# ScalarE takes a unit's root and a gate's copy of the combined projection ahead of the block's copy

## The chip, the cores and the metric

The kernel runs on one core of one Trainium2 chip. The metric is the device time of one launch, in microseconds (us). The engines are named TensorE (PE in the rows), VectorE (DVE), ScalarE (ACT), GpSimd (POOL) and SyncE (SP, which here only issues DMAs). PEld is TensorE's loading of weights.

## What is computed

One step of a trunk of two layers over 512 latent tokens and 128 prompt tokens, all in float32, with a width of 1024. The part that the change touches is the combined projection of a layer and what hangs on it:

```python
h = rms_norm(x, p['norm1_g'][l]) * (1 + scale1) + shift1
proj = h @ p['w_in'][l]
gq, gk, gv, gg, gaf, gab, cval, cgate, aq, ak, av = jnp.split(proj, ...)
la_f = jax.nn.log_sigmoid((gaf @ p['gla_a_w_f'][l] + p['gla_a_b_f'][l])) / GLA_NORMALIZER
la_b = jax.nn.log_sigmoid((gab @ p['gla_a_w_b'][l] + p['gla_a_b_b'][l])) / GLA_NORMALIZER
u = cval * jax.nn.sigmoid(cgate)              # then a depthwise convolution of 31 taps
qa = rms_norm(heads(aq, HEAD_DIM), p['q_norm_g'][l])
ka = rms_norm(heads(ak, HEAD_DIM), p['k_norm_g'][l])
...                                           # rotary on latent tokens, softmax attention
...                                           # gated linear attention by chunks of 64 tokens
```

After attention, the chunked linear attention and the convolution, an output projection and a gated residual follow, and then a mixture of single experts: each token picks 16 of 16384 experts in each of 8 heads, and the rows of these experts are gathered from two tables in memory.

## The kernel before

Each layer goes through four phases: projection with attention, chunked linear attention, output projection, expert stage. All four compute engines meet at the end of a phase (line 257); output projection and experts are one phase for this. Activations are kept transposed: 128 channels on the partitions and 640 tokens along the free dimension.

The projection is cut into 16 blocks of output columns, numbered 0 to 15 and listed in BLOCKS: the convolution's gate and value (blocks 0 to 3), the attention's key (block 4), its queries (5 to 8), the 32 columns of the two decay gates (9), the keys and queries of the linear attention (10 to 13) and its output gate (14, 15). For each block TensorE runs 16 matmuls into one of two pairs of PSUM banks, taken in turn. The trace has 32 records for them. Before block b it waits until ScalarE has evacuated block b-2 (proj_ev). All matmuls go through one helper, line 561, and so have that line in the profile; transposes are on lines 623 to 846.

Keys and queries form five units (UNITS, u = 0 to 4, which are blocks 4 to 8). Each is normalised per head and, for latent tokens, rotated. A unit's way goes through four engines and shares one buffer at each step:

- ScalarE squares it (line 1009, `square`), in round b = u + 4,
- TensorE averages the squares over each head (`variance`), behind the matmuls of block u + 5, into the first pair of banks. It waits for the square and, from unit 1 on, for the root of the unit before, which empties those banks,
- ScalarE takes the root (line 1015, `deviation`), in round b = u + 6. From unit 1 on it waits until VectorE has normalised the unit before (n_ready), because the roots share the tile SD,
- VectorE takes the reciprocal of the root and scales the unit (lines 1316 and 1317), which sets n_ready,
- TensorE multiplies it with the rotation matrix (`rotated`), behind block u + 7, and VectorE combines the two with cosine and sine (lines 1321 to 1323).

The four decay gates are matmuls of block 9 with a small matrix, behind the matmuls of blocks 11 to 14, into the same first pair of banks. Gate i waits, from the second on, until ScalarE has copied gate i - 1 with its bias (line 1029, z_ready), which it does in round 12 + i.

In layer 0 the blocks from 3 on are each followed by a chunk of the modulation, the product of the conditioning with 512 columns of a weight matrix. SyncE loads a slab of 2 MB for each: it waits until the chunk before is done (m_ps), then issues four DMAs (lines 349 and 350), and after ScalarE has copied the chunk's result (line 973) it writes it to memory in four small DMAs (line 361). For 4 of the chunks the result is turned into columns by TensorE instead, at the beginning of the next chunk, and copied by line 968. SyncE also loads the weights of block b + 3 when block b is done (line 367).

Beside this, VectorE and GpSimd run the two halves of the convolution, VectorE 18 of its taps before it turns to the units and the rest after them; GpSimd all of its taps in one go. After block 15 TensorE duplicates the keys into the layout of attention. It waits there for the last rotation, for the fourth gate's copy and, in layer 0, for the last chunk.

ScalarE runs everything in the order in which the code issues it. A round b of its loop in the projection (lines 1017 to 1035) is before the change: wait for the block's matmuls, copy of the block (line 1020), root, square, gate, and in layer 0 the chunk's result. Sigmoid, Sqrt and Silu each need another activation table than the one before; the table's load is an instruction of its own.

Of the kernel before, what the change touches and what calls it, by code (L numbers as in the profile page):

```python
# [9 lines left out]
ACT = mybir.ActivationFunctionType  # L10
# [7 lines left out]
NTOK = N_SAMPLE + N_PROMPT  # L18
# [26 lines left out]
def group_of(t):  # L45

    return 0 if t < NT_S else 1


def build(nc, x_prompt, x_sample, c, cache_k, cache_v, state_gla, c_ctx, ada_w, ada_b, norm1_g, norm2_g,  # L50
# [4 lines left out]
    with ctx:  # L55
# [3 lines left out]
        def sem(name):  # L59
            return ctx.enter_context(nc.semaphore(name))  # L60
# [133 lines left out]
        def pair(i):  # L194

            return PSF[:, 1024 * i:1024 * i + 1024]

        def zp(i):
# [4 lines left out]
        S = {n: sem(n) for n in (  # L203

            "const_in", "cond_in", "x_in", "adab_in", "gain1_in", "gain2_in", "gate_in", "mod2_in", "vec_in",
            "wv_in", "ck_in", "misc_in", "st_in", "keys_in", "wq_in",

            "cond_zero", "cond_ready", "m_ps", "m_row_done", "mod_out", "mc_ps", "mc_done", "mc_ready",

            "ss_done", "ms_done", "sd_done", "h_ready", "ht_ps", "ht_act", "ht_dve", "vec_ps", "vec_ready", "proj_ps",  # L210
            "proj_ev", "vt_ps", "vt_ready", "kc_ps", "kc_ready", "sq_ready", "var_ps", "sd_ready", "n_ready",
# [55 lines left out]
        NB = len(BLOCKS)  # L267
# [12 lines left out]
        def in_project(b):  # L280

            return b - FIRST_MOD if FIRST_MOD <= b < NB else None
# [20 lines left out]
        NU = len(UNITS)  # L303
# [649 lines left out]
        def _(act):  # L953
# [9 lines left out]
            def mod_rows(bank, n):  # L963

                if n - 1 in COLS:
                    c = n - 1 - COLS[0]
                    act.wait_ge(S["mc_ps"], WIDE + c + 1)
                    act.activation(mod_col[:, 1, 4 * c:4 * c + 4, :],
                                   PS[:, bank, 256:264].rearrange("p (j g) -> p j g", j=4), ACT.Copy)\
                        .then_inc(S["mc_done"], 1)  # L970
                act.wait_ge(S["m_ps"], WIDE + n + 1)
                act.wait_ge(S["mod_out"], 64 * stored(n))
                act.activation(m_chunk, PS[:, bank, 0:P], ACT.Copy).then_inc(S["m_row_done"], 1)

            def project(l):
                for t in range(NT):
                    st.link(act.activation(hbuf[:, t % 2, :], X[:, t, :], ACT.Square, accum_out=sumsq[:, 0, t:t + 1]))
                act.sem_inc(S["ss_done"], 1)
                act.wait_ge(S["ms_done"], l + 1)
                act.activation(rms[:, 0:NT], rstd[:, 0:NT], ACT.Sqrt).then_inc(S["sd_done"], 1)  # L980
                def h_out(t):
                    act.wait_ge(S["mc_ready"], l + 1)
                    act.wait_ge(S["ht_ps"], NT * l + t + 1)
                    for k in range(KT // 2):
                        c = mod_col[:, l, :, group_of(t)]
                        m = act.activation(HT[:, k, P * t:P * t + P], pair(t % 2)[:, P * k:P * k + P], ACT.Identity,
                                           bias=c[:, k:k + 1], scale=c[:, KT + k:KT + k + 1])
                    m.then_inc(S["ht_act"], 1)

                def vectors_out():  # L990
                    act.wait_ge(S["vec_ps"], l + 1)
                    act.activation(vec[:, :], PS[:, 4, 0:R_END], ACT.Copy).then_inc(S["vec_ready"], 1)
                    act.wait_ge(S["kc_ps"], l + 1)
                    act.activation(KC, PS[:, 5, 0:P], ACT.Copy).then_inc(S["kc_ready"], 1)

                if l:
                    vectors_out()
                for t in range(2):
                    h_out(t)
                if l == 0:  # L1000
                    vectors_out()
                for t in range(2, NT):
                    h_out(t)

                def square(u):
                    if u:
                        act.wait_ge(S["var_ps"], NU * l + u)
                    act.wait_ge(S["proj_ev"], NB * l + 4 + u + 1)
                    act.activation(SQ, UNITS[u][0], ACT.Square).then_inc(S["sq_ready"], 1)

                def deviation(u):
                    act.wait_ge(S["var_ps"], NU * l + u + 1)
                    if u:
                        act.wait_ge(S["n_ready"], NU * l + u)
                    act.activation(SD, pair(0)[:, 0:NTOK], ACT.Sqrt, bias=eps_c[:, 0:1]).then_inc(S["sd_ready"], 1)  # L1015

                for b, (dst, w, _c) in enumerate(BLOCKS):
                    act.wait_ge(S["proj_ps"], NB * l + b + 1)
                    f = ACT.Sigmoid if b in (0, 2) else ACT.Silu if b >= NB - 2 else ACT.Copy
                    act.activation(dst, pair(2 + b % 2)[0:w, 0:NTOK], f).then_inc(S["proj_ev"], 1)  # L1020
                    if 0 <= b - 6 < NU:
                        deviation(b - 6)
                    if 0 <= b - 4 < NU:
                        square(b - 4)
                    if b >= 12:
                        i = b - 12
                        col = (R_ABF if i < 2 else R_ABB) + i % 2
                        act.wait_ge(S["z_ps"], 4 * l + i + 1)
                        act.activation(LA[:, i, :], pair(0)[:, 0:NTOK], ACT.Identity, bias=vec[:, col:col + 1])\
                            .then_inc(S["z_ready"], 1)  # L1030
                    if b == 14:
                        act.wait_ge(S["kout_ps"], l + 1)
                        act.activation(KOUT, PS[:, 2, 0:P], ACT.Copy).then_inc(S["kout_ready"], 1)
                    if l == 0 and in_project(b) is not None:
                        mod_rows(3, in_project(b))
# [196 lines left out]
            for l in range(DEPTH):  # L1232
                project(l)
                attention(l)
                phase_end(act, PH * l + 1)
                gla(l)
                phase_end(act, PH * l + 2)
                out_project(l)
                peer(l)
                phase_end(act, PH * l + 3)  # L1240
# [390 lines left out]
```

## Time and profile before

| | us |
|---|---|
| median of 3 runs | 4506.6 |
| lowest and highest | 4503.03, 4546.3 |
| the profiled execution, time | 4498.38 |
| its span | 4496.2 |

| engine | busy us | share of the span |
|---|---|---|
| TensorE, matmuls | 2957.0 | 66% |
| TensorE, weight loads | 1278.9 | 28% |
| VectorE | 2770.1 | 62% |
| ScalarE | 966.7 | 21% |
| GpSimd | 2694.6 | 60% |

The chain that ended last is made of TensorE (25%), DMA (22%), issue (18%), VectorE (17%), GpSimd (15%) and ScalarE (2%). The mean granted clock of TensorE is 0.826 of full speed. In time, the start takes 54 us; the projection of layer 0 lasts from there to 260 us, that of layer 1 from 2318 to 2480 us. Attention and linear attention follow, and the expert stages lie from about 640 to 2300 us and from 2820 us to the end.

How to read the rows: a timeline gives start and duration in us, engine, line, operation, the names and shapes of output and inputs, the number of instructions merged into the row, and in brackets how long the engine was idle before it and who released it. Matmul ends are modelled.

### The profile page before, as it was taken

Reading aid. Unit: us, or ns where it says so; the run is one execution under the profiler, and the core shown is the slowest. Engines: PE = TensorE matmul, PEld = TensorE weight load, DVE = VectorE, ACT = ScalarE, POOL = GpSimd, SP = SyncE. Lnnn points to the kernel's source line nnn. Section 1 sums busy time; section 2 is a strip of 40 time slices with the busy share of each in tenths; the row PEclk is TensorE's granted clock in tenths of the full one; section 3 lists DMA queues with packets and bytes.
Section 4 is the critical chain, followed back from the end, with each engine's and each line's share of the span. In section 5 each row is a group of like instructions: output and inputs, shape, how many; then the busy total and the mean of one; then the engine's idle time right before and its main releaser. Section 6 shows DMA issues by size and latency. Waiting matters only on the chain.

```text
span 4496.2 us, 50088 instructions
## 1 busy us (share of the span) xinstructions
PE 2957.0 (66%) x17386; PEld 1278.9 (28%) x17386; DVE 2770.1 (62%) x6333; ACT 966.7 (21%) x2391; POOL 2694.6 (60%) x2762
## 2 busy tenths in 40 slices
PE   7999845556555555666578998455555556556655
PEld 4567521112221221222134674122212112112211
DVE  3516376677677677667536363766766776776673
ACT  2134111221122122222121422111212221222221
POOL 3700047777777777777748000677777777777775
PEclk9999778887887888777799978688878877888777
DMA  6532259999999999999941103999999999999998
GB/s 220 185 118 92 86 219 409 409 409 405 406 406 406 404 406 405 405 397 409 403 137 35 39 3 109 361 409 409 404 409 404 406 407 402 405 406 407 402 407 341
DMA packets 471181, 1450.20 MB, mean 323 GB/s; under 512 B 54165, under 2 KB 131345, under 8 KB 470801
## 3 DMA queue, kind: packets, MB, share of 16 engines
q0 software_dynamic: 368640, 1342.34, 75.4%
q1 hardware_dynamic: 102290, 104.66, 7.2%
q8 instruction: 140, 2.29, 0.2%
q14 instruction: 111, 0.91, 0.1%
HBM read 1443.62 MB, written 3.21 MB: 322 GB/s over the span
## 4 chain that ended last, share of the span: by engine, by line
PE 25%; DMA 22%; issue 18%; DVE 17%; POOL 15%; ACT 2%; DVEq 1%; SPq 1%; POOLq 0%; ACTq 0%
PE ps L561 24%; DMA arena<-in_peer_u,expert_rows 11%; DMA arena<-in_peer_v,expert_rows 10%; DVE arena L1506 8%; POOL arena L536 8%; POOL arena L544 7%; DVE arena L1454 1%; DVE top_indices L1453 1%; DVE arena L1485 1%; DVE arena L1488 1%; DVE chosen_pair L1490 1%; DVE top_values L1456 1%; DVE best_positions L1453 0%; DMA arena<-in_ada_w 0%; DVE top_indices L1458 0%
## 5 line engine op out<-in xcount | busy, mean ns | idle before, releaser
L561 PE MATMUL ps<-arena 64*64 64x512 f32 (+5 forms) x14768 | 2718.6, 674 | 1423.2 <-issue 1183.6
L1506 DVE CUSTOM_DVE_ANT_0 arena<-arena,ps 128x1024 f32<-128x1024 f32 x1280 | 1526.1, 1218 | 891.3 <-DMA arena<-in_peer_u,expert_rows 883.9
L561 PEld LDWEIGHTS ps<-arena 64*64 64x64 f32 (+2 forms) x14768 | 1121.0, 176 | 3006.7 <-issue 2896.0
L536 POOL DMA_INDIRECT arena<-in_peer_u,expert_rows x1280 | 1218.6, 952 | 688.3 <-issue 318.2
L544 POOL DMA_INDIRECT arena<-in_peer_v,expert_rows x1280 | 1205.9, 942 | 416.9 <-issue 357.9
L1219 ACT ACTIVATE arena<-constants,expert_weight 128x64 f32<-128x64 f32 x1280 | 380.3, 339 | 1370.2 <-PE ps L561 1346.4
L522 POOL MEMSET arena<- 128x4224 f32 x2 | 7.2, 3617 | 380.0 <-ACTq L257 380.0
L1334 DVE TENSOR_REDUCE score_max<-ps 128x1 f32<-128x640 f32 (+1 forms) x80 | 57.2, 716 | 224.5 <-PE ps L561 224.2
L515 POOL TENSOR_SCALAR arena<-arena,vec_columns 128x512 f32<-128x512 f32 x120 | 150.3, 1263 | 10.2 <-issue 10.2
L1146 ACT ACTIVATE arena<-ps 128x256 f32<-128x256 f32 x80 | 30.6, 383 | 477.3 <-PE ps L561 463.5
L1159 ACT ACTIVATE expert_gelu<-expert_act 128x16 f32<-128x16 f32 x80 | 17.3, 216 | 456.6 <-DVE expert_act L1506 456.6
L1506 DVE DVE_READ_ACCUMULATOR2_ANT expert_act<- 128x1 f32 x1280 | 104.3, 82 | 0.0
L518 POOL TENSOR_TENSOR arena<-arena 128x640 f32<-128x640 f32 x60 | 97.3, 1621 | 8.8 <-issue 0.2
L1154 ACT ACT_TABLE_LOAD x78 | 100.1, 1283 | 1.4
L561 PE MATMUL ps<-arena,constants 1*2 1x128 f32 (+3 forms) x404 | 79.9, 428 | 29.0 <-ACT arena L1015 15.4
L1159 ACT ACT_TABLE_LOAD x76 | 97.5, 1283 | 1.3
L525 POOL MEMSET arena<- 128x2048 f32 x2 | 3.6, 1805 | 156.2 <-DVEq L257 156.2
L1020 ACT ACTIVATE arena<-ps 128x640 f32<-128x640 f32 (+1 forms) x32 | 22.5, 702 | 273.9 <-PE ps L561 273.9
L1524 DVE TENSOR_TENSOR arena<-ps,arena 128x1024 f32<-128x1024 f32 x10 | 12.2, 1224 | 112.1 <-PE ps L561 112.1
L1046 ACT ACTIVATE arena<-ps,score_neg_max 128x640 f32<-128x640 f32 (+1 forms) x80 | 56.6, 708 | 108.1 <-DVE score_neg_max L1335 105.1
L1306 DVE SCALAR_TENSOR_TENSOR arena<-arena,vec_columns 128x512 f32<-128x512 f32 x120 | 78.3, 726 | 0.1
L1139 ACT ACTIVATE arena<-ps 128x128 f32<-128x128 f32 x80 | 22.1, 276 | 260.8 <-PE ps L561 250.9
(165 smaller groups left out, 1839.0 us busy)
## 6 DMA issues: line engine op xcount, KB each, us to landing
arena<-in_ada_w SPq DMA_DIRECT2D x40, 1024.0 KB
arena<-in_peer_u,expert_rows POOLq DMA_INDIRECT x1280
arena<-in_peer_v,expert_rows POOLq DMA_INDIRECT x1280
arena<-in_w_in SPq DMA_DIRECT2D x32, 512.0 KB, 4.1
arena<-in_ada_w SPq DMA_DIRECT2D x4, 2048.0 KB, 18.7
arena<-in_w_out SPq DMA_DIRECT2D x4, 2048.0 KB, 8.0
arena<-in_peer_wq SPq DMA_DIRECT2D x2, 4096.0 KB, 18.4
peer_modulation<-modulation_rows SPq DMA_DIRECT2D x4, 1536.0 KB, 11.1
```

Source lines behind the costliest of these rows:

```text
L515: pool.tensor_scalar(CV[:, 0, o:o + n], src, w, None, ALU.mult)
L518: pool.tensor_tensor(CX[:, 0, :], CX[:, 0, :], CV[:, 0, :], ALU.add)
L536: pool.indirect_dma_start(UR[:, k % RING, :], None, u_rows, bass.IndirectOffsetOnAxis(ap=rows[:, g % LIVE, k:k + 1], axis=0))\
L544: pool.indirect_dma_start(VR[:, k % RING, :], None, v_rows, bass.IndirectOffsetOnAxis(ap=rows[:, g % LIVE, k:k + 1], axis=0))\
L561: return pe.matmul(out, lhsT, rhs, start=start, stop=stop)
L1046: act.activation(PR[:, i % 2, 0:nk], pair(i % 2)[:, 0:nk], ACT.Exp, bias=nmax[:, i % 4:i % 4 + 1], scale=0.125, accum_out=psum_p[:, t % 2, ...
L1154: act.activation(gexp[:, g % LIVE, :], centred[:, :], ACT.Exp, accum_out=gsum[:, g % LIVE:g % LIVE + 1]).then_inc(S["exp_done"], 1)
L1159: act.activation(gelu_h[:, :], act_h[:, :], ACT.Gelu).then_inc(S["gelu_done"], 1)
L1219: act.activation(DG[:, k % DIAGS, :], eye2, ACT.Copy, scale=w_h[:, k:k + 1])\
L1306: st.do(stt(dst, src, w, dst, ALU.mult, ALU.add))
L1334: st.link(dve.reduce_max(smax[:, i % 4:i % 4 + 1], pair(i % 2)[:, 0:keys_of(t)[1]], AX.X))
L1506: dve.tensor_tensor_reduce(out=UR[:, k % RING, :], in0=UR[:, k % RING, :], in1=pair(1), scale=1.0, scalar=0.0, op0=ALU.mult, op1=ALU.add, ...
```

## The change

In each round of ScalarE's loop, the root (`deviation`) and the gate's copy now stand ahead of the wait for the block's matmuls and of the block's copy. The square stays behind the copy, as do the copy of the keys for output (round 14) and the chunk's result in layer 0. Nothing else in the kernel is touched: the same instructions run with the same waits of their own.

```diff
                 for b, (dst, w, _c) in enumerate(BLOCKS):
-                    act.wait_ge(S["proj_ps"], NB * l + b + 1)
-                    f = ACT.Sigmoid if b in (0, 2) else ACT.Silu if b >= NB - 2 else ACT.Copy
-                    act.activation(dst, pair(2 + b % 2)[0:w, 0:NTOK], f).then_inc(S["proj_ev"], 1)
                     if 0 <= b - 6 < NU:
                         deviation(b - 6)
-                    if 0 <= b - 4 < NU:
-                        square(b - 4)
                     if b >= 12:
                         i = b - 12
                         col = (R_ABF if i < 2 else R_ABB) + i % 2
                         act.wait_ge(S["z_ps"], 4 * l + i + 1)
                         act.activation(LA[:, i, :], pair(0)[:, 0:NTOK], ACT.Identity, bias=vec[:, col:col + 1])\
                             .then_inc(S["z_ready"], 1)
+                    act.wait_ge(S["proj_ps"], NB * l + b + 1)
+                    f = ACT.Sigmoid if b in (0, 2) else ACT.Silu if b >= NB - 2 else ACT.Copy
+                    act.activation(dst, pair(2 + b % 2)[0:w, 0:NTOK], f).then_inc(S["proj_ev"], 1)
+                    if 0 <= b - 4 < NU:
+                        square(b - 4)
                     if b == 14:
```

## Rows read from the trace of the kernel before

**Rows 1.** Table by stretch: length, busy of five engines (instructions), granted clock, DMA share, GB/s

```profile
2328.00:2362.00 34.00, 34.00 (x126) 18.91 (x125) 16.98 (x26) 3.36 (x5) 31.59 (x25) 1.00 0.24 62
2820.00:4496.00 1676.00, 985.88 (x5842) 322.91 (x5842) 1130.25 (x2700) 334.11 (x923) 1199.18 (x1267) 0.79 1.01 399
```

**Rows 2.** Waits in layer 0's projection: us in total, times, longest us

```profile
PE ps L561 <- ACT arena L1015: 7.7, 4, 3.0
...
PE ps L561 <- ACT arena L1029: 4.4, 3, 1.5
```

**Rows 3.** Timeline of TensorE, layer 1's projection

```profile
2374.18 1.32 PE L561 MATMUL ps<-arena,constants 128*128 128x512 f32 x4 [2.99 <-ACT arena L1015]
2375.33 8.82 PE L561 MATMUL ps<-arena 128*128 128x512 f32 x32
...
2398.11 2.18 PE L561 MATMUL ps<-arena,constants 128*128 128x512 f32 x6 [1.57 <-ACT arena L1015]
...
2410.57 2.18 PE L561 MATMUL ps<-arena,constants 128*128 128x512 f32 x6 [1.55 <-ACT arena L1015]
...
2443.53 1.34 PE L561 MATMUL ps<-arena,gla_gate_w 32*128 32x512 f32 x4 [1.48 <-ACT arena L1029]
...
2480.29 2.85 PE L561 MATMUL ps<-arena,constants 128*128 128x512 f32 x12 [1.52 <-issue]
```

**Rows 4.** Timeline of ScalarE, layer 1, blocks 6 and 7

```profile
2371.22 0.70 ACT L1020 ACTIVATE arena<-ps 128x640 f32<-128x640 f32 x1 [7.92 <-PE ps L561]
2371.94 1.28 ACT L1015 ACT_TABLE_LOAD   x1
2373.24 0.79 ACT L1015 ACTIVATE arena<-ps,eps_column 128x640 f32<-128x640 f32 x1
...
2384.78 0.79 ACT L1015 ACTIVATE arena<-ps,eps_column 128x640 f32<-128x640 f32 x1
```

**Rows 5.** Timeline of VectorE: layer 0, unit 1; layer 1, early taps and units 1, 2

```profile
151.94 0.88 DVE L1317 SCALAR_TENSOR_TENSOR arena<-arena,vec_columns 128x640 f32<-128x640 f32 x1
...
2348.26 22.80 DVE L1306 SCALAR_TENSOR_TENSOR arena<-arena,vec_columns 128x512 f32<-128x512 f32 x34
...
2395.14 0.89 DVE L1317 SCALAR_TENSOR_TENSOR arena<-arena,vec_columns 128x640 f32<-128x640 f32 x1
...
2408.03 0.89 DVE L1317 SCALAR_TENSOR_TENSOR arena<-arena,vec_columns 128x640 f32<-128x640 f32 x1
```

**Rows 6.** VectorE's line 1322, by source: shortest, median, longest ns

```profile
L1322 DVE TENSOR_TENSOR arena<-arena,constants x10: 680/940/1799, 145.0 to 2432.6; 128x512 f32<-128x512 f32 x10
```

**Rows 7.** Timeline of SyncE's queue and of TensorE: layer 0's slab at block 15

```profile
246.45 0.55 SPq L349 DMA_DIRECT2D arena<-in_ada_w  x1
...
256.61 0.39 PE L561 MATMUL ps<-constants,arena 128*128 128x8 f32 x2 [1.38 <-DMA arena<-in_ada_b]
```

**Rows 8.** Low clock: TensorE's timeline in layers 0 and 1, and the table by stretch

```profile
126.78 2.47 PE L561 MATMUL ps<-arena,constants 128*128 128x512 f32 x4 [2.99 <-ACT arena L1015]
129.18 2.25 PE L561 MATMUL ps<-arena,cond_silu 128*32 128x128 f32 x64
...
144.29 1.95 PE L561 MATMUL ps<-arena,cond_silu 128*32 128x128 f32 x64
...
146.50 8.92 PE L561 MATMUL ps<-arena 128*128 128x512 f32 x32
...
228.00 2.89 PE L561 MATMUL ps<-arena,cond_silu 128*32 128x128 f32 x64 [0.27 <-ACT modulation_columns L968]
...
231.35 9.35 PE L561 MATMUL ps<-arena 128*128 128x512 f32 x32
...
2468.37 10.40 PE L561 MATMUL ps<-arena 128*128 128x512 f32 x32
...
2469.00:2471.00 2.00, 2.00 (x5) 1.10 (x4) 0.00 (x0) 0.00 (x0) 0.00 (x0) 0.50 0.00 0
```

**Rows 9.** Waits over the whole span: us in total, times, longest us

```profile
POOL arena L522 <- ACTq L257: 380.0, 2, 219.1
```

## The prediction, made before the change was timed

> **What bounds the kernel now.** I read the page first: busy shares, the forty slices, the chain that ended last. No engine is busy for even seventy per cent of the span (TensorE 66%, the table above), so the stages have to be read one by one. The table by stage [rows 1] shows two kinds. The two expert stages (640 to 2300 us and 2820 to 4496 us) run with the DMA engines full, share 1.01 at 399 GB/s: nothing that ScalarE does in the projection changes their length, it can only move their start. The projections (54 to 260 us in layer 0, 2318 to 2480 us in layer 1) are another thing: where nothing interrupts it, TensorE is busy for 34.00 of 34 us. It sets their pace, and time comes back only where it stands still.
>
> So the next view is the waits of a projection [rows 2]. In layer 0 TensorE waited four times for the root of line 1015 (7.7 us) and three times for the gate's copy of line 1029 (4.4 us); in layer 1 the same two figures come again. The timeline of TensorE in layer 1 shows where they lie [rows 3]: 2.99 us after block 6, 1.57, 1.57 and 1.55 us after blocks 7, 8 and 9, and 1.48 us after each of blocks 12, 13 and 14. One more of 1.52 us stands ahead of the key duplication; the trace puts it on "issue", but the code waits there for the fourth gate's copy, and the length is that of a gate's copy behind a block's copy. ScalarE's own timeline [rows 4] gives what fills them: the block's copy starts when the block's last matmul is done (2371.22), then come the load of the root's table (1.28 us) and the root (0.79 us), and TensorE goes on 0.14 us later. From block 7 on there is no load: the root follows the copy's start by 0.60 us (2384.78 there), takes 0.79, and 0.14 later TensorE goes on. Before that copy ScalarE had been idle for 7.92 us, with the root's input already in PSUM.
>
> **The change, part by part.** No instruction is added or taken away, and no DMA is moved: SyncE waits for what TensorE finishes and for the rows of modulation, and both keep their place behind the block. 10 roots (5 a layer) and 8 gate copies go ahead of the copy of the block. Each can then run under the block's 32 matmul records, 8.8 us [rows 3].
>
> Root 0, block 6. Its input is ready when the variance behind block 5 ends, at about 2362.5 in layer 1. ScalarE then takes the square of unit 1 until 2363.3, the table load 1.28 and the root 0.79: done at 2365.4, against a block that ends at 2371.2. The whole 2.99 us goes, in both layers. The load stays single: behind it copies, squares and roots follow each other with no further one [rows 4], and only the identity of the gates changes place with them. VectorE, which divides by this root, is late next: in layer 1 it is in its early taps until 2371.06 [rows 5], so unit 0 is normalised by 2376.2 instead of 2379.1. Root 1 waits for that (it overwrites the tile that is read) and ends at 2377, still under block 7, which then ends at 2381.2: 1.57 us goes in both layers.
>
> Roots 2 and 3, blocks 8 and 9. Here a wait limits the gain: root u waits until unit u-1 is normalised, and that starts with a rotation on TensorE. In layer 1 unit 1 is normalised at 2395.14 + 0.89 = 2396.03 [rows 5]. The root would run at 2396.07 to 2396.86 and TensorE go on at 2397.00, not at 2398.11: 1.11 us goes, 0.46 us stays. For unit 2, 2408.03 + 0.89 = 2408.92, hence TensorE at 2409.89, not 2410.57: 0.68 us goes. In layer 0 a chunk of the modulation (2.3 us) stands between rotation and block: unit 1 is normalised at 151.94 + 0.88 = 152.82 [rows 5], block 8 ends at 155.4, and 1.57 and 1.55 us go whole. Root 4 holds nobody up. If VectorE were so late that nothing went at blocks 8 and 9, 1.11 + 0.68 + 1.57 + 1.55 = 4.9 us of the sum would be missing; that is this term's lower bound.
>
> What is queued behind the root is the block's copy, some 0.4 us late in layer 1. Who waits for it: the square of the same round, wanted a block later, and TensorE's block b+2, whose bank it frees, 11 us later (a block, a variance, a rotation). That is the cover.
>
> Gate copies, blocks 12 to 15. The gate's matmul is done right behind the block before, ScalarE is idle then, and the copy (0.79 us) lies under the next block. Three stalls of 1.48 us go in each layer. In layer 1 the fourth, 1.52 us, goes too. In layer 0 it does not exist: there TensorE waits at block 15 for a slab of modulation weights (1.38 us) and then for the evacuation of its result.
>
> That slab is what is late next in layer 0. It is asked for when the chunk before is done (246.45) and is there by 256.57, 10.1 us [rows 7]. The stretch that has to cover it is 8.92 + 1.34 = 10.26 us at blocks 12 to 14 once the gate's stall is gone, and 8.92 + 1.25 = 10.17 us at block 6. So I count nothing for it; if each slab took 0.6 us more, four stalls of about 0.5 us came back, 2 us.
>
> Sum of the stalls: layer 0, 2.99 + 4.69 + 4.44 = 12.12 us; layer 1, 2.99 + 1.57 + 1.11 + 0.68 + 4.44 + 1.52 = 12.31 us; together 24.4 us.
>
> The clock. Three times in the projections the granted clock fell to 0.50, that is 1.2 instead of 2.4 GHz, for 2 to 4 us, each time just behind one of these stalls [rows 8]: at 127 us behind the 2.99, at 229 us behind a 1.48 and a 0.27, at 2469 us behind a 1.48. The price, against the same work at full clock: variance 2.47 for 1.25 and chunk 2.25 for 1.95, 1.52 us; chunk with its biases 231.35 - 228.00 = 3.35 for 146.50 - 144.29 = 2.21 and block 9.35 for 8.92, 1.57 us; block 10.40 for 8.82, 1.58 us. Together 4.7 us. The stretch without a stall shows 1.00 [rows 1], so I take all of it; the other end is nothing, since layer 1's 2.99 us had no fall behind it. By the rows the sum is 24.4 + 4.7 = 29.1 us. The Trainium skill ("TensorE: Matmul & The Clock Gate", What's actually happening) says that what sets the clock runs free of the kernel, so that the place of a slow spell differs from run to run. By that rule the spells need not go with their stalls, and the sum stays at 24.4 us.
>
> Behind the projection the gain must be carried some 4,200 us in layer 0 and 2,000 us in layer 1. In attention GpSimd isn't the bound: it waits 380 us at the two ends of that phase [rows 9]. The slabs of layer 0 are each asked for when the one before is used, and the gathers start when routing is done. All of it moves with TensorE; I find nothing that is fixed in absolute time.
>
> The sum is made on the profiled execution (span 4496.2, time 4498.4): 4498.4 - 29.1 = 4469 us. The median of the runs shown is 8 us above it: 4506.6 - 29.1 = 4477.5, so 4478 us.
>
> **The rivals.**
> (A) VectorE and the slabs keep part: nothing goes at blocks 8 and 9, slabs come 0.6 us later, and the spells stay. For it: the same operation of VectorE takes between 0.68 and 1.80 us [rows 6]. Against: layer 0 has 155.4 - 152.8 = 2.6 us to spare. 24.4 - 4.9 - 2 = 17.5 us: 4489 us. Chance 0.17.
> (B) The spells of the low clock stay, the stalls go: 24.4 us, 4482 us. For it: one stall of 2.99 us had none behind it. Against: each of the three had a stall before it. Chance 0.2.
> (C) The end doesn't move: a later wait that I don't see takes what is gained, 4500 to 4510 us. For it: the chain that ended last runs 22% on DMA. Against: no such wait in the rows. Chance 0.1.
> (D) Slower: the copy is held behind the root. Place: blocks 7 to 10, where the root waits for VectorE. It costs nothing until the copy is 10 us late, when TensorE can't enter block b+2; from there each microsecond costs one at eight blocks. From rotation to normalised takes 8.1 us; with the 1.1 us that line 1322 varies by [rows 6] on each of its five operations 13.6, and the copy 6 us late. To lose 1% (45 us, and the 29 forgone: 74 over eight blocks) it would have to be 19 us late: 4552 us. Chance 0.02. The Trainium skill ("TensorE: Matmul & The Clock Gate", Architectural detail) calls ScalarE's queue a strict FIFO. By that rule every late root delays its copy, and the trace agrees as far as line 1020's copies and line 1015's roots start in the order of the code.
> (E) More: the state updates, whose clock is low for a part, fall better. 10 us more, 4468 us. Chance 0.06.
> The forecast, 27 to 31 us, has the rest, 0.45.
>
> **How the numbers follow.** About 1% is what a measurement of this kernel can tell from no change. Forecast, (B), (A) and (E) lie between 4468 and 4489 us, with 0.88 of the chance; the three runs before reach 4 us below their median and 40 above, so I put the upper end at 4508, which takes in most of (C), and the lower at 4467. Faster by over 1% (below 4461.5) is (E) taken further, 0.04. Slower by over 1% is (D) and a little of (C), 0.03. Within 1%: 0.93.
>
> **What would show it.** In the profile after: TensorE's waits for the root go from 7.7 us to nothing in layer 0 and to 1.1 us or less in layer 1, at blocks 8 and 9 alone; those for the gate's copy go to nothing; the 1.52 us ahead of the duplication is gone. From block 0 to the duplication layer 0 is 12 to 15 us shorter, layer 1 12 to 14. The root's table load lies inside block 6, VectorE's reciprocal of unit 0 follows its early taps without a gap in layer 1, and the clock is 1.00 throughout the projections. Wrong would be: a wait of TensorE for line 1020, more than two loads for the root, stalls on slabs longer by over 2 us, or projections that are 24 us shorter with an end that isn't.

## The result

| | before | after |
|---|---|---|
| median of 19 runs, us | 4503.03 | 4464.43 |
| lowest and highest | 4494.11, 4547.63 | 4458.09, 4509.47 |
| profiled execution, time | 4498.38 | 4462.68 |
| its span | 4496.2 | 4460.4 |

The ratio is 0.9912, with a 95% interval of 0.9885 to 0.9939: 0.9% faster, some 39 us. The forecast was 4478 us in a range of 4467 to 4508. The direction was right, "within 1%" too, but the time lies 2.6 us under the range: the gain is a third larger than the 29.1 us of the sum.

Executions of every kernel here without bridges (below) fall into two groups, 41 to 45 us apart and 9 to 20 us wide. Of the 109 runs of the kernel before that were timed beside the others, 75 and 34 are in them, with medians 4501.2 and 4542.4 us; of the 33 of the changed one 23 and 10, 4461.7 and 4506.6 us. The kernel before was also run 20 times in its own two repeats: 11 and 8 more, which would make the medians 4500.7 and 4541.5 us, and one of 8124.68 us at a mean clock of 0.396 that is left out. Below, "short group" is the lower one, and kernels are compared in it: 4501.2 - 4461.7 = 39.5 us is what has to be explained.

### The profile page after: what moved, and what is told of

The parts are those of the page before. It is cut to its first block, busy times and chain, and to the rows that moved or that the text cites. A ratio compares the mean times of both kernels' runs of the same rounds, so it can differ in the third digit from the quotient of the medians.

```text
span 4460.4 us, 50088 instructions
## 1 busy us (share of the span) xinstructions
PE 2962.0 (66%) x17386; PEld 1272.4 (29%) x17386; DVE 2771.3 (62%) x6333; ACT 968.2 (22%) x2391; POOL 2706.9 (61%) x2762
## 4 chain that ended last, share of the span: by engine, by line
PE 24%; DMA 22%; DVE 18%; issue 17%; POOL 15%; DVEq 1%; ACT 1%; SPq 1%; POOLq 0%; ACTq 0%
PE ps L561 23%; DMA arena<-in_peer_u,expert_rows 12%; DMA arena<-in_peer_v,expert_rows 10%; DVE arena L1506 8%; POOL arena L536 8%; POOL arena L544 8%; DVE arena L1454 1%; DVE top_indices L1453 1%; DVE arena L1485 1%; DVE arena L1488 1%; DVE chosen_pair L1490 1%; DVE top_values L1456 1%; DVE best_positions L1453 0%; DMA arena<-in_ada_w 0%; DVE top_indices L1458 0%
## 5 line engine op out<-in xcount | busy, mean ns | idle before, releaser
L515 POOL TENSOR_SCALAR arena<-arena,vec_columns 128x512 f32<-128x512 f32 x120 | 153.4, 1289 | 10.2 <-issue 10.2
L561 PE MATMUL ps<-arena,constants 1*2 1x128 f32 (+3 forms) x404 | 76.9, 417 | 13.4 <-ACT arena L1227 11.6
L1524 DVE TENSOR_TENSOR arena<-ps,arena 128x1024 f32<-128x1024 f32 x10 | 12.2, 1225 | 111.8 <-PE ps L561 111.8
```

The source lines that it names most:

```text
L515: pool.tensor_scalar(CV[:, 0, o:o + n], src, w, None, ALU.mult)
L561: return pe.matmul(out, lhsT, rhs, start=start, stop=stop)
```

## The profile after

The stages, from the timelines, in us. Projection is from block 0's first matmul to the duplication; attention from there to the phase's end.

| | before | after | difference |
|---|---|---|---|
| start, layer 0 | 54.2 | 54.0 | -0.2 |
| projection, layer 0 | 205.9 | 190.8 | -15.1 |
| attention, layer 0 | 166.4 | 167.1 | +0.7 |
| linear attention, layer 0 | 81.7 | 81.6 | -0.1 |
| output projection and experts, layer 0; norm of layer 1 | 1801.2 | 1799.9 | -1.3 |
| projection, layer 1 | 171.0 | 159.2 | -11.9 |
| attention, layer 1 | 146.3 | 146.5 | +0.2 |
| linear attention, layer 1 | 84.1 | 77.0 | -7.2 |
| output projection and experts, layer 1 | 1785.5 | 1784.5 | -1.0 |

The projection of layer 1 starts at 2309.3 us in the kernel before, not at 2318 as the text ahead of the prediction has it.

So 27 us came from the two projections, where the sum had 29.1, and 7 us from a stage that the change does not touch. Everything else is carried unchanged, as the prediction had it. In this pair of profiles the clock gave next to nothing in the projections: before, it is low for 10.2 us behind stalls; after, it is low for 9.2 us at the start of block 0, in both layers together.

TensorE's timeline in layer 1's projection, which answers to [rows 3]:

```profile
2358.12 1.25 PE L561 MATMUL ps<-arena,constants 128*128 128x512 f32 x4
2359.20 8.82 PE L561 MATMUL ps<-arena 128*128 128x512 f32 x32
2367.86 2.10 PE L561 MATMUL ps<-arena,constants 128*128 128x512 f32 x6
2369.80 8.81 PE L561 MATMUL ps<-arena 128*128 128x512 f32 x32
2379.50 2.18 PE L561 MATMUL ps<-arena,constants 128*128 128x512 f32 x6 [0.88 <-ACT arena L1015]
...
2390.89 2.18 PE L561 MATMUL ps<-arena,constants 128*128 128x512 f32 x6 [0.48 <-ACT arena L1015]
...
2412.02 1.34 PE L561 MATMUL ps<-arena,gla_gate_w 32*128 32x512 f32 x4
...
2422.14 1.34 PE L561 MATMUL ps<-arena,gla_gate_w 32*128 32x512 f32 x4
...
2452.47 2.77 PE L561 MATMUL ps<-arena,constants 128*128 128x512 f32 x12
```

Of the eight idle times two are left, 0.88 and 0.48 us behind blocks 8 and 9. The prediction had 0.46 and 0.87 there: 1.36 us against 1.33, with the two changed round. ScalarE's timeline for the same blocks, which answers to [rows 4]:

```profile
2350.43 1.28 ACT L1015 ACT_TABLE_LOAD   x1
2351.72 0.79 ACT L1015 ACTIVATE arena<-ps,eps_column 128x640 f32<-128x640 f32 x1
2358.32 0.70 ACT L1028 ACTIVATE arena<-ps 128x640 f32<-128x640 f32 x1 [5.81 <-PE ps L561]
...
2378.56 0.80 ACT L1015 ACTIVATE arena<-ps,eps_column 128x640 f32<-128x640 f32 x1 [8.68 <-DVE arena L1317]
2379.25 0.70 ACT L1028 ACTIVATE arena<-ps 128x640 f32<-128x640 f32 x1
```

The table load and root 0 are over 5.8 us before the block is. Root 2 now waits for VectorE's normalisation (line 1317) and the block's copy (line 1028 here) is queued behind it, and nobody waits for that copy. VectorE's timeline says why root 2 was 0.4 us later than forecast: from its first product behind the rotation (line 1321) to the unit normalised it took 8.47 us, and 8.10 before. Its sum of line 1323 took 1.91 us here and 1.06 before, line 1322 took 0.68 and 1.28.

```profile
2371.33 1.91 DVE L1323 TENSOR_TENSOR arena<-arena 128x512 f32<-128x512 f32 x1
2373.27 4.15 DVE L1316 RECIPROCAL arena<-arena 128x640 f32<-128x640 f32 x1
2377.46 1.01 DVE L1317 SCALAR_TENSOR_TENSOR arena<-arena,vec_columns 128x640 f32<-128x640 f32 x1
```

In layer 0's projection (waits: us in total, times, longest) both rows of [rows 2] are gone. ScalarE's root waits for VectorE instead, under the block, and of TensorE's waits that for the slabs is left:

```profile
ACT arena L1015 <- DVE arena L1317: 15.2, 3, 5.1
...
PE ps L561 <- DMA arena<-in_ada_b: 1.3, 2, 0.7
```

They are 1.3 us where they were 1.8. The one at block 15 is 0.68 us where it was 1.38 [rows 7], the one behind block 4 is 0.63 where it was 0.41: the slabs cost no more than before.

And the stage that was not in the sum, layer 1's linear attention between its last gaps; first before, then after (stretch, busy of the five engines, granted clock, DMA share, GB/s):

```profile
2665.50:2674.70 9.20, 9.16 (x96) 7.69 (x96) 5.87 (x7) 0.00 (x0) 0.00 (x0) 1.00 0.01 2
2674.70:2676.70 2.00, 0.05 (x3) 0.02 (x1) 1.96 (x5) 0.70 (x1) 0.00 (x0) 0.87 0.00 0
2676.70:2699.00 22.30, 22.30 (x128) 18.80 (x128) 8.46 (x12) 2.14 (x4) 0.00 (x0) 0.50 0.00 1
```

```profile
2637.40:2646.60 9.20, 9.16 (x96) 7.68 (x96) 5.88 (x7) 0.00 (x0) 0.00 (x0) 1.00 0.02 4
2646.60:2648.60 2.00, 0.05 (x3) 0.02 (x1) 1.97 (x5) 0.70 (x1) 0.00 (x0) 1.00 0.00 0
2648.60:2657.80 9.20, 9.18 (x96) 7.67 (x96) 5.88 (x7) 0.13 (x1) 0.00 (x0) 1.00 0.01 2
2657.80:2664.30 6.50, 4.57 (x32) 3.90 (x32) 2.50 (x6) 2.01 (x3) 0.00 (x0) 0.77 0.00 0
```

The same gap on TensorE's timeline, one row of before, two of after:

```profile
2676.68 22.47 PE L561 MATMUL ps<-arena 128*128 128x64 f32 x128 [1.95 <-DVE arena L1430]
```

```profile
2648.59 9.19 PE L561 MATMUL ps<-arena 128*128 128x64 f32 x96 [1.95 <-DVE arena L1430]
2659.73 4.66 PE L561 MATMUL ps<-arena 128*128 128x64 f32 x32 [1.95 <-DVE arena L1430]
```

Both kernels do the same 96 matmuls in 9.2 us and then wait 1.95 us for VectorE. Before, the clock falls in that gap to 0.50 (1.2 GHz), and the remaining 128 matmuls take 22.3 us. After, it stays at full over this gap and falls 1.7 us behind the next of the same size; 96 of the 128 take 9.2 us. From the end of the first gap to the matmuls of 512 columns that follow it was 22.4 us and is 15.7 (the second gap included): that is 6.7 of the 7.2 us.

## The experiments

Two aids are used in several kernels. "Filled" means that matmuls whose result nobody reads run in the projection's stalls; "bridged" means that such matmuls run in three later gaps of TensorE, one in layer 0's attention and two in the linear attention. Both keep TensorE busy; what it waits for stays the same.

Short group medians in us, with the number of runs in both groups. The short group median of before was between 4500.5 and 4502.2 us in each of the five sets of runs timed beside the others, so kernels of different sets can be compared to some 2 us:

| kernel | short group | long group | against before |
|---|---|---|---|
| before | 4501.2 (75) | 4542.4 (34) | |
| changed | 4461.7 (23) | 4506.6 (10) | -39.5 |
| roots only | 4481.8 (9) | 4526.2 (3) | -19.4 |
| gates only | 4479.9 (7) | 4524.1 (5) | -21.3 |
| changed, roots 2 and 3 behind | 4465.4 (10) | 4509.8 (2) | -35.8 |
| before, stalls filled | 4489.4 (9) | 4534.1 (3) | -11.8 |
| before, bridged | 4487.7 (12) | none | -13.5 |
| before, filled and bridged | 4486.2 (12) | none | -15.0 |
| changed, bridged | 4455.6 (11) | none | -45.6 |

### Both kernels once more

No edit.

> The kernel before, unchanged, as a measure of what differs with nothing changed. The projections got 27 us shorter in the profiles (layer 0 205.9 to 190.8 us, layer 1 190.4 to 178.4 us from its first square to the duplication) and 7.2 us more came from layer 1's linear attention (84.1 to 77.0 us between the two phase ends), where TensorE's clock stayed at 1.00 for 96 more matmuls. Theory 1 (chance): where the clock falls in that stage is drawn anew in each execution, so this profile can show either length, 77 or 84 us, and the medians' difference of some 39 us must have another source. Theory 2 (fixed): the kernel before has 84 us there always, and this profile shows 83 to 85 again. Ratio to itself 0.998 to 1.002.

> The changed kernel, unchanged. Ratio 0.991 again (4462 against 4502 us). Theory 1 (chance): layer 1's linear attention may be 77 or 84 us in this profile. Theory 2 (fixed): 76 to 78 us again. Projections as in the first profile: 190.8 and 178.4 us within 1.5 us.

Measured: 4503.99 us (ratio 1.000, 0.996 to 1.004) and 4466.01 us (0.994, 0.991 to 0.997; in the short group the difference is 39.1 us, and was 40.2 in the first timing). Linear attention of layer 1 was 83.9 and 77.0 us, as in the first profiles. The profile of the kernel before fell into the long group this time, and shows what that group is. Its attention in layer 0 took 39 us longer, and the linear attention behind it 2.8 us. Attention by stretch:

```profile
256.00:360.00 104.00, 101.61 (x914) 70.33 (x907) 31.01 (x57) 40.50 (x75) 0.00 (x0) 1.00 0.40 131
360.00:372.00 12.00, 9.59 (x105) 7.31 (x108) 5.29 (x10) 4.91 (x10) 0.00 (x0) 0.81 0.35 116
372.00:460.00 88.00, 87.71 (x316) 68.20 (x313) 38.12 (x74) 24.22 (x60) 0.00 (x0) 0.50 0.13 48
```

```profile
368.38 3.64 PE L561 MATMUL ps<-arena,cond_silu 128*32 128x128 f32 x64 [2.41 <-ACT arena L1058]
```

The clock falls once, at 367 us, in a gap of 2.41 us in which TensorE waits for ScalarE to evacuate the bank that a modulation chunk will use, and it does not come back for the rest of the stage, although TensorE is busy for 87.71 of the 88 us. The changed kernel's first profile had the same gap (at 354 us), the same fall, and full clock again 3 us later. The long group is this one fall: of the ten profiles without bridges four are of the long group, and these four have it with the clock low for 99 to 102 us, while in the other six it is not there or over after 3 us.

### Roots alone, gates alone

```diff
-copy; root; square; gate
+root; copy; square; gate          (roots only)
+gate; copy; root; square          (gates only)
```

> Only the roots go ahead of the block's copy; the gate's copy stays behind it. By the stalls counted in the profile before: layer 0 2.99 + 4.69, layer 1 2.99 + 1.57 + 1.11 + 0.68, together 14.0 us, and 1.5 us for the clock's spell behind root 0: 15.5 us less than before, ratio 0.9966. TensorE's wait for the gate's copy stays at 4.4 us a layer, its waits for the root fall to nothing and to about 1.1 us. Rival (the roots' gain is kept back by VectorE): under 9 us. Rival (the 7 us of linear attention come with the roots): 22 us, with layer 1's linear attention at 77 us.

> Only the gate's copy goes ahead of the block's copy; the roots stay behind it. By the stalls counted: 2 x 4.44 + 1.52 = 10.4 us and 3.2 us for the two spells of low clock behind gates: 13.5 us less than before, ratio 0.997. TensorE's waits for the root stay at 7.7 us a layer. Rival (spells of low clock aren't tied to the stalls): 10.4 us, with a clock under 1.00 somewhere in blocks 11 to 15. Rival (the 7 us of linear attention come with the gates): 20 us, with that stage of layer 1 at 77 us. If roots and gates are independent, the two gains add up to that of the whole change.

Measured: ratios 0.9947 (0.991 to 0.998) and 0.9961 (0.992 to 1.000), 19.4 and 21.3 us in the short group. The two add up to 40.7 against 39.5 for both, so they are independent as far as a spread of some 2 us lets one tell. Each is more than its stalls and spells (15.5 and 13.5). The waits are as expected: with the roots alone TensorE still waits 4.4 us a layer for the gate's copy, with the gates alone 7.7 us for the root. Apart from block 0, the clock fell twice in the projections of each: with the roots alone both times behind a gate's stall, with the gates alone both times behind the 2.99 us. Linear attention in layer 1 was 83.8 us with the roots and 77.0 us with the gates, which looks like a cause; the next experiment speaks against it.

### Roots 2 and 3 behind the copy

```diff
-                    if 0 <= b - 6 < NU:
+                    if 0 <= b - 6 < NU and b not in (8, 9):
                         deviation(b - 6)
...                  # wait and copy of the block
+                    if b in (8, 9):
+                        deviation(b - 6)
```

> The changed kernel with the roots of units 2 and 3 (blocks 8 and 9) back behind the copy. By the stalls counted they gave 1.57 + 1.55 us in layer 0 and 1.11 + 0.68 us in layer 1, so this kernel is 4.9 us slower than the changed one, 4467 us in the short group, with TensorE waiting 1.57 us at blocks 8 and 9 in both layers. Rival (VectorE keeps the gain): as fast as the changed kernel, 4462 us.

Measured: 3.7 us slower than the changed kernel in the short group; 4.9 were expected, within the spread. TensorE's two waits are back at 1.57 and 1.55 us. This profile also answered another question: gates ahead, and yet linear attention of layer 1 at 84.3 us. So that stage is not tied to the order of gates.

### The stalls filled, and the bridges

The fills are the first two hunks, the bridges the last two. In layer 0 each fill first waits until ScalarE has copied the last chunk's result out of the bank that it writes:

```diff
                     if u:
+                        fill(u + 5, 5 if u == 1 else 2)   # n matmuls of 512 columns
                         pe.wait_ge(S["sd_ready"], NU * l + u)
...
+                            fill(b, 2)
                             pe.wait_ge(S["z_ready"], 4 * l + i)
...
+                        if i == 20:
+                            for _ in range(5):
+                                mm(PS[:, 6, 128:512], ident, cos_t[:, 0:384])
...
+                    if s in (5, 9):
+                        keep_busy(2 if s == 5 else 3, 3)
                     if s >= 1:
                         gla_out(l, s - 1)
```

> The changed kernel with matmuls whose result nobody reads in three places where TensorE stands still while its clock is at full: 5 of 384 columns in layer 0's attention, step 20, in the gap of 2.4 us ahead of a modulation chunk; and 3 of 512 columns, ahead of the product of steps 4 and 8, in the two gaps of 1.95 us in both layers' linear attention. Theory: those gaps are where the clock falls. In the attention it falls in some executions and stays at 0.50 for 96 us (a second group of times, 40 us longer: 6 of 19 runs of the changed kernel, 15 of 35 of the kernel before); in the linear attention it falls at the first gap (82 to 85 us from phase end to phase end) or at the second (77 us). Bridged: no run in the long group, linear attention 73 to 74 us in both layers, so 4451 us where the changed kernel has 4462, ratio to before under 0.985 with the long group gone. Rival: the fall is tied to the small matmuls around the gap, not to the gap. Then nothing changes, 4462 and 4506 us.

> The kernel before with the same bridges. Theory: what the change gave beyond the projections (39 us between the medians of the short groups, against 27 to 32 us in the projections) came from the clock in the linear attention, 84 us in three profiles with the gates behind the copy and 77 us in three with the gates ahead. With the bridges both kernels have 73 to 74 us there, so this kernel should run in 4501 - 8 - 10.5 = 4483 us, and the difference to the bridged changed kernel should be 30 to 32 us. Rival: the difference stays 39 us, so the projections give more than the stalls and spells counted.

> The kernel before, with matmuls whose result nobody reads put into the projection's stalls: 5 of 512 columns ahead of the wait for root 0, 2 ahead of each wait for roots 1 to 3 and for gates 0 to 2. The stalls stay as long as they are, but TensorE is busy for most of each. It separates the clock's term from the stalls' own. By the spells (4.7 us, three falls of the clock behind stalls): granted clock 1.00 in both projections, 4.7 us shorter than before, 4497 us in the short group. Rival (spells fall anywhere): a clock under 1.00 somewhere in the projections all the same, and 4501 us.

> The bridged changed kernel once more, for more executions on the same chip as the next one: 4458 us again, no execution in the long group (over 4490 us). If the bridges only had luck, one in three executions should be near 4500 us.

> The kernel before with both: the projection's stalls filled with matmuls whose result nobody reads, and the bridges in attention and linear attention. What is left between it and the bridged changed kernel is the stalls alone. In profiles, with the time of low clock taken off, the projections are 202.5 and 169.3 us long before and 189.2 and 156.0 us after, 26.5 us less, where the idle times summed to 24.4; the fills add some 1.5 us a layer. So theory 1 (stalls alone): 26.5 to 29.5 us slower than the bridged changed kernel, 4486 us, and about as fast as the bridged kernel before (4487.6) less its low clock in the projections. Rival (the idle times in the trace overstate, the clock did it): under 22 us, below 4480 us.

The bridges: none of the 35 runs of the four bridged measurements is in the long group, where 34 of 109 of the kernel before are. In its profile the changed, bridged kernel has full clock where the fall was:

```profile
340.00:370.00 30.00, 29.91 (x295) 22.44 (x294) 16.33 (x29) 11.62 (x24) 0.00 (x0) 1.00 0.50 165
```

Linear attention is 76.3 to 78.3 us in both layers and all four profiles. The expected 73 to 74 us was wrong: the clock still falls near the end of the stage (2664.6 us in the first of them). So both kernels came out slower than expected, 4458.6 for 4451 us and 4487.7 for 4483. With that stage alike, the two kernels are 4487.7 - 4455.6 = 32.1 us apart (29.1 by the runs timed side by side); 30 to 32 were expected, and 39 us by the rival.

The stalls filled: clock 1.00 throughout both projections, in this profile and in that of the filled, bridged one. The four profiles of kernels with all stalls (before three times, and bridged) have three or four falls each behind a stall, the five with none (changed three times, bridged twice) have none; the one other place is block 0, where six profiles, of either kind, start at low clock in one layer or both.

```profile
54.50:258.50 204.00, 201.07 (x1537) 113.95 (x1538) 80.63 (x89) 29.42 (x51) 124.77 (x94) 1.00 0.54 167
2308.60:2479.40 170.80, 169.28 (x594) 89.47 (x594) 81.83 (x89) 25.14 (x34) 128.27 (x94) 1.00 0.15 39
```

The falls do belong to the stalls. But the time of the filled kernel went down by 11.8 us, not by 4.7, although the fills themselves cost time. Its profiled execution, 4495.8 us, is among the longer ones of a short group that reaches from 4481.5 to 4497.3, so what the shorter ones saved can't be read from it; that it is the linear attention is likely by the next figure, and not shown. With the bridges, where linear attention can't differ, filling the stalls gave 4487.7 - 4486.2 = 1.5 us, and the fills cost about 1.5 us a layer (layer 1: 170.8 us against 169.3 without low clock), so the clock's term in the projections is 4.5 us. By the profiles it is larger: half of the time at low clock behind stalls is 5.1, 6.8, 5.1 and 10.2 us in the four. What is left between filled, bridged before and bridged after is the stalls: 4486.2 - 4455.6 = 30.6 us, less 3.0 for the fills, 27.6. Between runs timed side by side the two differences of the bridged kernels are 4487.7 - 4458.6 = 29.1 and 4486.2 - 4454.4 = 31.8, so each of these terms is known to some 2 us.

### The third profiles

> The kernel before, one more profile, for what decides the linear attention of layer 1: 84 us in four profiles of kernels with stalls in the projection, and in one without; 77 us in three with the gates ahead. If it is decided anew each time, with odds that the change shifts, either length can come. If it is tied to the stalls, 84 us again.

> The changed kernel, one more profile. If tied to the stalls: 77 us in layer 1's linear attention, as in its first two profiles, projections of 189 to 191 and 156 to 159 us. If decided anew each time: either length.

Measured: 84.1 and 76.9 us in layer 1's linear attention, projections of the changed kernel as expected. The profile of before was again of the long group, with 204.0 us of attention in layer 0. The changed kernel was timed only twice here (ratio 0.985, 0.972 to 0.998), which is too few to weigh.

## Why the prediction missed, point by point

- **The path.** Right. TensorE sets the pace of the projection, its stalls are where the time comes back, and the stages behind carry the gain. Rivals (C) and (D) did not occur: TensorE waits for the copy's line in no projection of the changed kernel.
- **The stalls, 24.4 us.** Undersized by some 2 us. With low clock taken off (half of the time that it lasts), the projections are 202.5 and 169.3 us before (202.5 and 202.5, 169.3 and 169.3 in the first two profiles) and 189.2 and 156.0 us after: 26.5 us. The sum took each stall at the idle time that the trace prints. From variance to variance over block 7 it was 2385.72 - 2374.18 = 11.54 us and is 2367.86 - 2358.12 = 9.74: 1.80 us gone, not 1.57. From gate to gate 11.67 became 2422.14 - 2412.02 = 10.12: 1.55, not 1.48. Matmul ends are modelled, and a stop costs more than the gap between two rows. In layer 0 the slab's stall at block 15 shrank by 0.7 us too.
- **Roots 2 and 3 held by VectorE.** Right: 1.36 us of stalls are left in layer 1 and none in layer 0, and undoing the two cost 3.7 us where 4.9 was counted. The sum had left 0.46 + 0.87 = 1.33 us; the sign that the prediction named, "1.1 us or less", didn't fit its own sum.
- **The slabs.** Right that they stay hidden.
- **The clock in the projection, 4.7 us.** Right in cause: no fall with the stalls filled, and none in the projections without a stall ahead of it but at block 0. The size is near: 4.5 us by the fills under bridges, known to some 2 us, and 5 to 10 us by the single profiles. The sign "1.00 throughout the projections" did not hold in the first profile after, for block 0's sake. The choice between the rows' 4.7 and the rule's nothing came out for the rows: by the Trainium skill ("TensorE: Matmul & The Clock Gate", What's actually happening) the place of a spell differs between runs, and the traces agree with that, since the stall behind which it falls differs from profile to profile; but none fell in the projection's later blocks where there was no stall.
- **The linear attention, not in the sum.** This is the step that failed: "Behind the projection the gain must be carried", with the clock of the state updates left to rival (E) at 0.06. In the short group it is worth 39.5 - 32.1 = 7.4 us on average (10 by the bridged runs timed side by side), and 7.2 us in the profiles. The table by stage had shown the clock at half there; how much of the stage hangs on one gap of 1.95 us was not worked out.
- **The range.** Its lower end stood 10 us under the forecast, for (E) alone. The stalls that were 2 us too small and the linear attention took that up, and the median of before, with three runs, had stood 3.6 us too high. Of the 13.1 us from 4477.5 to 4464.4 us, 3.6 are that median, some 2 the stalls and some 7 the linear attention.

## What the linear attention hangs on, and what stays open

Ten profiles without bridges, layer 1: the time from the clock's last rise to the start of the first gap of 1.95 us, and the stage's length.

| kernel | rise to gap | length |
|---|---|---|
| before, three profiles | 12.2, 12.3, 12.1 | 84.1, 83.9, 84.1 |
| roots only | 12.4 | 83.8 |
| stalls filled | 12.3 | 83.9 |
| roots 2 and 3 behind | 11.9 | 84.3 |
| changed, three profiles | 12.6, 12.6, 12.9 | 77.0, 77.0, 76.9 |
| gates only | 12.7 | 77.0 |

Some tenths of a microsecond separate the profiles in which the clock falls in the first gap (up to 12.4) from those in which it falls behind the second (from 12.6). The order of gates and roots is some 200 us earlier. In the profiles the odds are shifted (4 of 5 with the gates ahead are short, none of 5 with them behind); by which chain the change would do so isn't shown, and with ten profiles chance can't be excluded either. That the gain is there on average rests on the 7 to 10 us by which the bridges brought the two kernels nearer.

## What to carry to other kernels

An in-order engine that waits for the busiest one should do whatever is already ready before that wait, if nobody needs the work behind the wait at once: here two blocks of cover made it free, and the idle times in the trace gave three fifths of the gain. A gap in TensorE's work has a second price in the clock, and that price may fall due in another stage: look at each gap of some 2 us in a stretch of small matmuls before summing. The bridged version of the changed kernel, at 4455.6 us and without the long group, is faster than both kernels (ratios 0.990 and 0.988 to before).

## What the runs showed of the hardware

- One gap of 2.41 us, after over 100 us at full clock, put TensorE at half clock for the following 102 us. For 88 of these the profile shows it 99% busy, mostly with matmuls of 64 and 128 columns. It happened in about 3 of 10 executions and cost some 42 us. With five matmuls in the gap it happened in none of 35.
- The clock also fell at gaps of 1.95 us (linear attention of layer 1, 10 of 10 profiles without bridges: six in the first such gap, four 1.3 to 1.7 us behind the second) and behind stalls of 1.48 us.
- The idle time that the trace prints between TensorE's rows is less than what came back when a stop was gone altogether: 0.07 us less at a stop of 1.48 and 0.23 us less at one of 1.57.
